# Score products of the first two mixers with zero-padded keys over 128 rows instead of 64-row slices

## The reference, cut to what matters

```
q = rope(rms_norm(q))                          # 8 heads of 64, 256 tokens
k_slc, k_win = rope(rms_norm(k))               # 2 groups of 64, each shared by 4 query heads
s_s = q . k_slc * scale ; s_w = q . k_win * scale      # "slc" and "win": 8 heads each
p = masked_softmax(s, causal) ; o = p @ v
q, k = rope(rms_norm(q)), rope(rms_norm(k))    # moba: 8 heads of 64, each with its own key
s_own = q . k * scale ; p = masked_softmax(s_own, causal) ; o = p @ v
```

## Time and profile before

| | |
|---|---|
| time, median of 3 runs | 2040.02 us (2039.95 to 2040.09) |
| span of the profiled execution, first to last instruction | 2037.8 us |
| time outside the span, by the median | 2.2 us |
| TensorE matmuls busy | 1996.7 us, 98% |
| TensorE weight loads busy (beside the matmuls) | 1774.0 us, 87% |
| VectorE busy | 1466.3 us, 72% |
| ScalarE busy | 1092.8 us, 54% |
| GpSimd busy | 23.6 us, 1% |
| granted TensorE clock, mean | 0.999 of full speed |

### The profile page before, as it was taken

The page is one execution under the profiler, slowest core; times in us unless marked ns, Lnnn a source line. Parts: engine busy times, 40 slices in busy tenths (PEclk is TensorE's granted clock), DMA queues, the critical chain, the costliest instruction groups (busy, mean ns, idle before and its releaser), DMA issues. The chain is left out here.

```text
span 2037.8 us, 32169 instructions
## 1 busy us (share of the span) xinstructions
PE 1996.7 (98%) x12934; PEld 1774.0 (87%) x12934; DVE 1466.3 (72%) x2326; ACT 1092.8 (54%) x1732; POOL 23.6 (1%) x46
## 2 busy tenths in 40 slices
PE   7999999999999999999999999999999999999999
PEld 5889988898789988898888779888898899899888
DVE  7887778857787786567757577677667757767774
ACT  3555555535656455545546666555455537855552
POOL 1001000000010000000000000000000000000000
PEclk9999999999999999999999999999999999999999
DMA  9455558765455576555556423455555544235553
GB/s 352 159 200 197 188 186 270 263 211 184 166 203 192 165 234 201 184 188 186 186 175 202 140 101 127 145 186 186 184 186 186 187 167 137 94 125 166 186 176 135
DMA packets 266212, 372.23 MB, mean 183 GB/s; under 512 B 8400, under 2 KB 160336, under 8 KB 266064
## 3 DMA queue, kind: packets, MB, share of 16 engines
q1 hardware_dynamic: 264736, 368.91, 54.1%
q10 hardware_dynamic: 1328, 1.26, 0.2%
HBM read 369.09 MB, written 1.05 MB: 182 GB/s over the span
## 5 line engine op out<-in xcount | busy, mean ns | idle before, releaser
L2302 DVE TENSOR_TENSOR parts<-ring,parts 128x2048 fp32r<-128x2048 f32 (+2 forms) x304 | 676.0, 2224 | 390.7 <-ACT parts L721 390.1
L721 ACT ACTIVATE parts<-ring 128x2048 fp32r<-128x2048 f32 (+2 forms) x304 | 565.5, 1860 | 554.1 <-PE psum L1513 321.6
L1513 PE MATMUL psum<-h,parts 128*128 128x512 f32 x1920 | 676.2, 398 | 0.0
L1511 PE MATMUL psum<-h,parts 128*128 128x256 f32 x1920 | 539.3, 281 | 0.7 <-DVE parts L2302 0.4
L1513 PEld LDWEIGHTS psum<-h,parts 128*128 128x128 f32 x1920 | 361.1, 188 | 87.3
L1511 PEld LDWEIGHTS psum<-h,parts 128*128 128x128 f32 x1920 | 362.4, 189 | 2.4 <-DVE parts L2302 2.2
L1505 PE MATMUL psum<-h,parts 128*128 128x256 f32 (+1 forms) x2088 | 265.0, 285 | 4.5 <-DVE h L2311 2.0
L1505 PEld LDWEIGHTS psum<-h,parts 128*128 128x128 f32 (+1 forms) x2088 | 254.0, 190 | 7.2 <-issue 4.9
L1505 PE MATMUL psum<-parts,h 128*128 128x512 f32 (+1 forms) x864 | 203.3, 386 | 5.7 <-DVE h L2311 3.3
L1505 PE MATMUL psum<-hid_hl,parts 128*128 128x256 f32 x1584 | 189.3, 282 | 0.8 <-DVE parts L2302 0.6
L1505 PEld LDWEIGHTS psum<-hid_hl,parts 128*128 128x128 f32 x1584 | 187.9, 189 | 2.4 <-DVE parts L2302 2.4
(11 more groups left out here) (265 smaller groups left out, 2119.3 us busy)
## 6 DMA issues: line engine op xcount, KB each, us to landing
ring<-in_w_ffn_in SPq DMA_DIRECT2D x88, 512.0 KB, 4.8
ring<-in_ffn_w_gate SPq DMA_DIRECT2D x88, 512.0 KB, 3.7
ring<-in_ffn_w_up SPq DMA_DIRECT2D x88, 512.0 KB, 4.7
ring<-in_w_ada SPq DMA_DIRECT2D x43, 1024.0 KB, 5.4
ring<-in_w_in SPq DMA_DIRECT2D x36, 1024.0 KB, 5.0
ring<-in_ffn_w_down SPq DMA_DIRECT2D x32, 1024.0 KB, 5.0
ring<-in_w_ffn_out SPq DMA_DIRECT2D x16, 1024.0 KB, 5.2
ring<-in_ffn_w_down SPq DMA_DIRECT2D x16, 768.0 KB, 4.4
```

The source lines that it names most:

```text
L721: act.activation(out, in_, func, **kw).then_inc(*sig(name, *keys))
L1511: pe.matmul(bank[:, 0:S], wt_hl[1], act[:, 0, :], start=start, stop=False, skip_group_check=True)
L1513: return pe.matmul(bank.rearrange("p (a s) -> p a s", a=2), wt_hl[0], act, start=False, stop=stop, skip_group_check=True)
L2302: dve.tensor_tensor(out, a, b, op).then_inc(*sig(name, *keys))
```

## The change

The score products of the 24 heads of each first-block layer contract over all 128 partitions. The queries are used as they lie, with both heads of the pair. Each key gets a copy of its own over 128 partitions: its 64 rows hold the key and the other 64 rows hold zeros, so the other head's query rows add nothing. Keys of group 0 and of even moba heads have zeros below, the others above. The key areas double: ks_pad takes the place of ks_t and kw_t, kw_pad has a new buffer, and the odd moba keys take 1024 columns of feat from 5856 on, where the compressed branch keeps v_diag, cmp_s and cmp_pt until its last product. The zeros are written by GpSimd: those of kw_pad once at the start, the others in each layer behind the tables. ScalarE moves each key in two copies of 64 partitions instead of one of 128 (half_copies).

```
-        ks_t, kw_t, kc_t = feat[:, 1024:1280], feat[:, 1280:1536], feat[:, 1536:1568]
+        kc_t = feat[:, 1536:1568]
+        ks_pad, kw_pad = (a.rearrange("p (g s) -> p g s", g=2)
+                          for a in (feat[:, 1024:1536], kw_area[:]))
-        mk_t = feat[:, 2624:3648].rearrange("p (j s) -> p j s", s=S)
+        mk_pad = [feat[:, a:a + 1024].rearrange("p (j s) -> p j s", s=S) for a in (2624, 5856)]
...
-                        n=n, q=nq_t[HD * g:HD * g + HD, j, :], k=k_t[HD * g:HD * g + HD, :],
+                        n=n, q=nq_t[:, j, :], k=k_pad[:, g, :],
...
-            return [dict(n=n, q=q_t[HD * (n % 2):HD * (n % 2) + HD, n // 2, :],
-                         k=k_t[HD * (n % 2):HD * (n % 2) + HD, n // 2, :],
+            return [dict(n=n, q=q_t[:, n // 2, :], k=k_pad[n % 2][:, n // 2, :],
...
+            pool.memset(kw_pad[HD:P, 0, :], 0.0).then_inc(*sig("pool_zeros"))
+            pool.wait_ge(*own("pool"))
+            pool.memset(kw_pad[0:HD, 1, :], 0.0).then_inc(*sig("pool_zeros"))
+            pool.wait_ge(*own("pool"))
             pool.wait_ge(*at("loaded rows"))
...
                 table(4, trig[0:16, 1, 2:3, :], trig[0:16, 0, 2:3, :], row("nsa_k_gain", HD, l),
                       HD, ("kc", l), 16)
+                if l:
+                    pool.wait_ge(*at(("x", ("ffnout", l - 1), DC - 1)))
+                else:
+                    for panel in ADA_OUTSIDE:
+                        pool.wait_ge(*at(("released", panel)))
+                pool.wait_ge(*own("pool"))
+                pool.memset(ks_pad[HD:P, 0, :], 0.0).then_inc(*sig("pool_zeros"))
+                pool.wait_ge(*own("pool"))
+                pool.memset(ks_pad[0:HD, 1, :], 0.0).then_inc(*sig("pool_zeros"))
+                pool.wait_ge(*own("pool"))
+                pool.memset(mk_pad[0][HD:P], 0.0).then_inc(*sig("pool_zeros", ("key zeros", l)))
+                pool.wait_ge(*own("pool"))
+                pool.wait_ge(*at(("full", ("cmp out", l, 1))))
+                pool.memset(mk_pad[1][0:HD], 0.0).then_inc(
+                    *sig("pool_zeros", ("odd key zeros", l)))
+                pool.wait_ge(*own("pool"))
...
+            def half_copies(job, even, odd):
+
+                act.wait_ge(*at(("full", job)))
+                for half, dst in enumerate((even, odd)):
+                    r = slice(HD * half, HD * half + HD)
+                    n = dst.shape[1] * (dst.shape[2] if len(dst.shape) == 3 else 1)
+                    src = psum[r, tally.bank(job), 0:n]
+                    if len(dst.shape) == 3:
+                        src = src.rearrange("p (a b) -> p a b", b=S)
+                    run(dst[r], src, ACT.Copy, "act_copied",
+                        *([("copied", job), ("free", job)] if half else []))
...
-                copies(("tr ks", l), ks_t)
+                act.wait_ge(*at(("key zeros", l)))
+                half_copies(("tr ks", l), ks_pad[:, 0, :], ks_pad[:, 1, :])
...
-                        copies(("tr kw", l), kw_t)
+                        half_copies(("tr kw", l), kw_pad[:, 0, :], kw_pad[:, 1, :])
...
                     if i == 15:
+                        act.wait_ge(*at(("odd key zeros", l)))
                         for j in range(2):
-                            copies(("tr mk", l, j), mk_t[:, 2 * j:2 * j + 2, :])
+                            half_copies(("tr mk", l, j), *(a[:, 2 * j:2 * j + 2, :]
+                                                           for a in mk_pad))
```

More of the change, by code:

```diff
@@ L315, in build @@
         qk_gain = sb("qk_gain", [MQ, 1])
+        kw_area = sb("kw_area", [P, 2 * S])
         subln_gain = sb("subln_gain", [P, 1])
@@ L510, in nsa_heads @@
         def nsa_heads(kind):
-            k_t, c_v = (ks_t, C_VS) if kind == "slc" else (kw_t, C_VW)
+            k_pad, c_v = (ks_pad, C_VS) if kind == "slc" else (kw_pad, C_VW)
             first = 4 if kind == "slc" else 6
@@ L521, in nsa_heads, with paired @@
             return out
-        def paired(q_t, k_t, v):
-            return [dict(n=n, q=q_t[HD * (n % 2):HD * (n % 2) + HD, n // 2, :],
-                         k=k_t[HD * (n % 2):HD * (n % 2) + HD, n // 2, :],
+        def paired(q_t, k_pad, v):
+            return [dict(n=n, q=q_t[:, n // 2, :], k=k_pad[n % 2][:, n // 2, :],
                          v=[v[:, t, HD * n:HD * n + HD] for t in range(TT)],
@@ L558, in attention_of @@
             if kind == "moba":
-                return paired(mq_t, mk_t, tok_in[:, :, C_VB:C_BR]), con("causal"), HD ** -0.5
+                return paired(mq_t, mk_pad, tok_in[:, :, C_VB:C_BR]), con("causal"), HD ** -0.5
             if kind == "diff":
```

## The result

The change made the kernel slower: 2044.31 us (median of 20 runs, 2039.62 to 2049.95) against 2040.05 us for the kernel before, run beside it (20 runs, 2037.81 to 2041.64). The ratio is 1.0018, with a 95% interval of 1.0012 to 1.0024. I had forecast 2033.8 us with a range of 2029.0 to 2037.0, so the time lies outside, on the other side. The runs of the change also spread over 10.3 us, those of before over 3.8, and they spread with the clock: the fastest had a mean granted TensorE clock of 0.997, the slowest 0.992.

A forecast was written before the change was run, and what follows sets the result against it. TensorE, busy 98% of the span, was taken as the bound, held at places by ScalarE and VectorE; 3.2 + 3.0 us off the 2037.8 span gives 2031.6, plus 2.2 around it 2033.8 us, range 2029.0 to 2037.0.

The forecast's parts named there:

- The price of a head: First-block head steps on TensorE: full-height scores save 0.35 us entering from the projection, 0.31 for six heads a layer.
- ScalarE as what TensorE newly waits for before head 16: Scores of head 16: TensorE newly waits 1 to 2 us for ScalarE's moba key copies.
- the zeros at nothing: GpSimd's memsets of zeros beside other work: taken as 0 us; a rival had them slower, 2047.0 us, chance 0.05.
- VectorE near the end of the layers: Near each layer's end: TensorE newly waits about 1 us for VectorE's part.
- the low part that I had named: End of layer 0: VectorE's last low part, early by about 3.0 us, taken by TensorE with 0.16 to spare.
- Heads 0 to 6: nothing: First heads of each layer: TensorE waits for ScalarE's compressed copies, so 0 gained, bounds -0.3 and +0.3 us.
- the window keys' second copy: Step 1, before the compressed keys: one ScalarE copy becomes two, 0.3 us more, paid back by heads 3 and 4.
- tr ks: Key copy before head 0: gains a half, but ScalarE idles before its next work, so 0 us.
- the moba copies, 0.98 us more: ScalarE's moba key copies before head 16: two in 1.06 us become four, half a microsecond each.
- VectorE's chain: Heads 10 to 16: VectorE's work without pause, then ScalarE's moba copies, leave head 16 early by 1.5 us in layer 0.
- The cap by VectorE: Heads 10 to 14: VectorE has no pause, so what follows can be early by 1.8 us at most.
- TensorE decides alone: Rival, whole first block: VectorE and ScalarE have hidden room, full 5.8 us a layer gained, 2028.4 us, chance 0.14.

The follow-up runs named there:

- run 5: The changed kernel with run 1's reordering, plus ScalarE's exponential of the compressed scores put behind its evacuation of the next window panel: 2026.31 us, ratio 0.9932.
- run 9: The kernel before, scores on 64 rows, with all five moves of run 5 in ScalarE's order: 2035.46 us, ratio 0.9978.
- run 1: The changed kernel with four ScalarE copies earlier (compressed keys before window keys, compressed probabilities before transposed ones, moba keys before head 15's exponentials): 2028.45 us, ratio 0.9943.
- run 7: The changed kernel with only the moba keys copied ahead of the exponentials of head 15: 2035.66 us, ratio 0.9979.
- run 2: The kernel before, scores on 64 rows and whole copies, with the same four copies earlier as in run 1: 2036.44 us, ratio 0.9987.
- run 4: The kernel before with three needless ScalarE copies of 128x384 ahead of its copy of the compressed keys: 2051.84 us, ratio 1.0059.
- run 8: The kernel before with one needless ScalarE copy of 128x384 ahead of the compressed keys: 2042.31 us, ratio 1.0014.

## Why the prediction was wrong

**Right.** The price of a head: 0.35 us foretold, 0.35 measured in a plain step, with the gap behind the scores gone. So were ScalarE as what TensorE newly waits for before head 16, and the zeros at nothing where the trace was compared. VectorE near the end of the layers is right in part: TensorE waits for it there (0.54 and 0.33 us in layer 0), but for its mask of head 23 and for a step on the heads' outputs (y), not for the low part that I had named. The Trainium skill's rule to cut the array in two when the contraction is 64 ("TensorEngine Tiling (Array Packing)", "When to Use Tiling") was not tried: no run here puts two 64-row products side by side. Against a 64-row product that stands alone, as these do, filling the rows with zeros gains 9.2 us (runs 5 and 9).

**Wrong, first: "Heads 0 to 6: nothing", with bounds of 0.3 either way.** I priced the window keys' second copy at 0.3 us, let heads 3 and 4 pay it back, and left out that TensorE gets there sooner by what heads 0 to 2 save. But these add at a wait: TensorE is there sooner, ScalarE later. The copy's cost was 0.41, that of "tr ks" 0.40 (I had called it hidden; 0.23 us of idle time was all that stood behind it, in front of ScalarE's next copy), and the wait grew by 1.5 us in each layer. The wait at 99.68, which I had in the rows, should have told that any delay on ScalarE's side shows in full. By the scores of head 7, where the forecast has TensorE at its old time, it was 2.3 us late in layer 0, the half clock behind the wait included.

**Wrong, second: the moba copies, 0.98 us more.** They took 1.37 more, since four copies of 64x512 follow each other every 0.61 us, not every 0.53. I had foretold a wait of 1 to 2 us there and measured 2.2 and 1.9, so this step was mis-sized rather than missed: the path that I gave for it, VectorE's chain and behind it ScalarE's copies, is the one that the trace shows (below).

**Wrong, third and largest: the clock was in no term.** The rows of before stood at 0.999 and I took that as given, with no bound for what a longer wait does to it. Its price in the profiled execution is up to 10.2 us, as much as all longer waits together (10.0). Without it the sum above gives 2040.05 + 10.0 - 12.6, about 2037 us, and the 20 runs point the same way: they took about 2040.8 us at a mean clock of 0.997 and 2049.4 at 0.992, a line that meets 0.999 near 2037. By this estimate the clock is some 7 of the 10.5 us by which the forecast missed, the waits the rest. A bound was to be had from the trace of before: its one fall, 3.4 us at 1214 us, stands behind a TensorE wait of 2.34 us in the second block. Its timeline there, and the microsecond behind with the clock at 0.50:

```profile
1213.02 0.67 PE L2093 MATMUL psum<-rot,const 128*128 128x256 f32 x2 [2.34 <-DVE rot L2302]
```

```profile
1214.00:1215.00 1.00, 1.00 (x8) 1.00 (x6) 0.96 (x2) 0.00 (x0) 0.00 (x0) 0.50 0.00 0
```

**The cap by VectorE held in the change, and run 1 lifted it.** I had let TensorE be early by 1.8 us at most at head 16, because VectorE has no pause from head 10 to 14. From its mask of head 10 to that of head 15 VectorE took 26.6 us before (143.20 to 169.79), 26.3 in the change (144.43 to 170.76) and 26.3 in run 5 (139.71 to 166.03), while TensorE's scores of these heads moved from 26.0 us apart to 24.5 in both. So VectorE was late for ScalarE's exponentials of head 15, and through them for the moba copies behind: that is the 1.25 us of the wait at head 16 which the copies' own 1.37 do not explain. In runs 1, 5 and 7 the copies stand ahead of these exponentials, and TensorE does not wait at head 16, though in run 5 VectorE gained as little: the chain was a bound through the order of ScalarE's copies, not by itself.

**The rival "TensorE decides alone", 2028.4 us, comes near runs 1 and 5 (2028.45 and 2026.31) partly by luck.** It has 11.6 us from the padding alone; measured are 8.0 (run 1 against 2) and 9.2 (run 5 against 9), and the rest of these runs' gain is the order's. From the scores of head 7 to those of head 23 a layer gained 5.0 us in run 5 against run 9.

## What to carry to other kernels

Shortening the engine that is busy all the time also shortens the time that the others have for each handover: list every place where it already waits, or nearly does, and add its earliness and the other side's new work there, with the same sign. Where the bound engine is TensorE, price a new wait of the lengths seen here (1.5 to 2.4 us) not at its length alone but with a possible half clock behind it, and look at the granted clock before reading any busy share. A change that comes out slower may need only an order: here five moves within ScalarE's order turned 4 us lost into 14 won, 4.3 of which the order gives without the change (run 9).

## What the runs showed of the hardware

- **The clock behind a wait is not certain.** Over the profiled executions of the kernels here there are 16 single waits of TensorE of 1.49 to 2.35 us between the heads: behind nine of them the granted clock fell to 0.50, for 3.4 or 10.2 us, behind seven it stayed at 1.00, equal waits of one execution among both (run 4). Behind 18 waits of 0.89 to 1.33 us there it never fell, and nowhere between the heads did it fall without one of the longer waits. But length is not all: in the projections of layer 1 it fell twice behind 0.66 and 0.63 us (runs 4 and 8). That the change, which has four of the longer waits, spreads over 10 us together with its clock fits this.
- **Half copies cost as much as whole ones.** ScalarE moves 128x512 from PSUM in 0.53 us when two follow each other, and 64x512 in 0.61 (2.43 for four); 64x256 took 0.385 (0.77 for two) where one 128x256 took 0.36 (0.38 at "tr ks"). The time of these goes by columns, not by partitions, and the half copies don't gain from following each other: each starts 0.60 us or more behind the last, the whole ones 0.48. The Trainium skill, "ScalarE: Activation LUTs", section "What ACT_TABLE_LOAD costs", says that back-to-back activations overlap; the whole copies agree with it, the half copies here don't.
- **A memset on GpSimd is cheap**: 0.31 us for 64x256 and 0.95 for 64x1024, where I had allowed up to 2.2 and 8.8.
